# Expert rows gathered before the last scatter has landed, attention scores two units ahead, loads begun a stage early, and two scan states

## The reference

```python
# block one, chunks of 128 tokens: y = C @ (decayed state) + masked (C B^T * decay) @ (x dt)
states = einsum("bclgn,bcgrl,bclgrp->bcgrpn", bm, decay_states, xdt)
def step(h, inp):
    s, d = inp
    return h * d[..., None, None] + s, h        # the scan over chunks
y_diag = einsum("bcgls,bcgrls,bcsgrp->bclgrp", cb, lmat, xdt)
y_off = einsum("bclgn,bcgrpn,bcgrl->bclgrp", cm, prev, exp(a_cs))
# conformer: layer norm over 1024 channels: mean, variance, scale, silu
# block two, attention: softmax of the masked scores and a sink, per block of 128 queries
scores = where(valid, einsum('bnqgrd,bnkgd->bngrqk', q, kb) * HEAD_DIM**-0.5, NEG_INF)
out = einsum('bngrqk,bnkgd->bnqgrd', softmax(concat([scores, sink]))[..., :-1], vb)
h = layer_norm(DEEPNORM_ALPHA * x + concat([attn, sgu]) @ w_out + b_out)
# routed experts: rows sorted by expert into blocks of 128
x_rows = concat([xt, 0])[row_tok].reshape(n_blocks, 128, D)
def expert_block(xb, e):
    gt = minimum(xb @ w_gate[e] + b_gate[e], 7)
    up = clip(xb @ w_up[e] + b_up[e], -7, 7)
    hid = gt * sigmoid(1.702 * gt) * (up + 1.0)
    return hid @ w_down[e] + b_down[e]           # then weighed by the gate and summed per token
x = layer_norm(DEEPNORM_ALPHA * h + ffn)
```

## Time and profile before

| What | Value |
|---|---|
| Median of 3 runs | 3385.69 us (3377.62 to 3389.89) |
| The profiled execution | 3407.19 us |
| Its span | 3405.5 us |
| Mean granted TensorE clock | 0.962 of full speed |
| Busy share: TensorE, VectorE, ScalarE, GpSimd | 93%, 79%, 54%, 22% |
| Moved from and to HBM | 810 MB and 59 MB |

### The profile page before, as it was taken

One profiled execution on the slowest core, in us unless ns is written; L12 is line 12 of the kernel. 1 busy time (PEld: TensorE's weight loads), 2 busy tenths in 40 slices (PEclk: granted clock), 3 DMA queues, 4 the chain that ended last, 5 costly groups with the idle time before them and its releaser, 6 DMA issues. The chain is left out here.

```text
span 3405.5 us, 47872 instructions
## 1 busy us (share of the span) xinstructions
PE 3155.6 (93%) x16432; PEld 2732.6 (80%) x16432; DVE 2677.4 (79%) x3834; ACT 1822.1 (54%) x2211; POOL 750.4 (22%) x465
## 2 busy tenths in 40 slices
PE   7999788999887999999998958899999999999997
PEld 7996777999887888888887846787888788777775
DVE  6885552994596878887887555899999999999996
ACT  4432442334585333333333342677787777777774
POOL 0000002446211445454454000111111111111111
PEclk9999789999998999999999969899999999999998
DMA  5221031334457999999997113889999999999995
GB/s 143 71 75 38 1 124 66 136 118 170 179 204 274 335 349 350 348 349 345 347 328 274 72 53 136 334 333 347 363 359 358 356 356 369 341 356 364 342 359 201
DMA packets 195751, 853.26 MB, mean 251 GB/s; under 512 B 21776, under 2 KB 104336, under 8 KB 151936
## 3 DMA queue, kind: packets, MB, share of 16 engines
q1 hardware_dynamic: 167712, 700.86, 56.1%
q0 software_dynamic: 27936, 151.02, 10.9%
HBM read 810.39 MB, written 59.24 MB: 255 GB/s over the span
## 5 line engine op out<-in xcount | busy, mean ns | idle before, releaser
L3148 DVE TENSOR_TENSOR moe_w_lo<-all_raw,moe_w_hi 128x2048 fp32r<-128x2048 f32 x298 | 676.9, 2287 | 64.7 <-ACT moe_w_hi L3075 62.3
L3075 ACT ACTIVATE moe_w_hi<-all_raw 128x2048 fp32r<-128x2048 f32 x298 | 568.5, 1915 | 83.5 <-PE moe_GU L3014 60.1
L3014 PE MATMUL moe_GU<-moe_w_hi,moe_x_lo 128*128 128x512 f32 x1056 | 412.3, 390 | 0.0
L3013 PE MATMUL moe_GU<-moe_w_lo,moe_x_hi 128*128 128x512 f32 x1056 | 412.2, 390 | 0.0
L3012 PE MATMUL moe_GU<-moe_w_hi,moe_x_hi 128*128 128x512 f32 x1056 | 411.9, 390 | 0.0
L1230 POOL TENSOR_TENSOR score_w_lo<-all_hT,score_w_hi 128x1024 fp32r<-128x1024 f32 x67 | 165.3, 2468 | 673.6 <-DVE all_x_lo L1346 531.4
L1855 DVE SCALAR_TENSOR_TENSOR experts_pair<-experts_pair,all_x_first 128x1024 f32<-128x1024 f32 x128 | 156.2, 1220 | 133.3 <-DMA experts_pair<-in_peer_pairs,experts_slot 133.3
L1699 POOL DMA_INDIRECT experts_pair<-in_peer_pairs,experts_slot x128 | 225.1, 1759 | 114.7 <-POOL experts_slot L1696 110.1
L3013 PEld LDWEIGHTS moe_GU<-moe_w_lo,moe_x_hi 128*128 128x128 f32 x1056 | 198.8, 188 | 42.2
L3014 PEld LDWEIGHTS moe_GU<-moe_w_hi,moe_x_lo 128*128 128x128 f32 x1056 | 198.6, 188 | 41.6
L3012 PEld LDWEIGHTS moe_GU<-moe_w_hi,moe_x_hi 128*128 128x128 f32 x1056 | 199.0, 188 | 40.6
(11 more groups left out here) (542 smaller groups left out, 8077.3 us busy)
## 6 DMA issues: line engine op xcount, KB each, us to landing
all_raw<-in_w_moe SPq DMA_DIRECT2D x149, 2048.0 KB, 9.1
all_hT<-in_w_moe SPq DMA_DIRECT2D x49, 2048.0 KB, 9.4
all_hT<-in_peer_wdT SPq DMA_DIRECT2D x128, 512.0 KB, 5.4
all_wu<-in_peer_pairs SPq DMA_DIRECT2D x64, 1024.0 KB, 13.8
peer_gates<-gates_out SPq DMA_DIRECT2D x6, 4096.0 KB
experts_gt<-peer_gates SPq DMA_DIRECT2D x32, 768.0 KB
all_hT<-in_w_in SPq DMA_DIRECT2D x40, 512.0 KB, 4.4
all_hid<-peer_early SPq DMA_DIRECT2D x60, 192.0 KB
```

Source lines behind the costliest of these rows:

```text
L3013: pe.matmul(out, x_hi[:, kx, :], lo[:, k, :], start=False, stop=False)
L3014: mm = pe.matmul(out, x_lo[:, kx, :], hi[:, k, :], start=False, stop=(kx == KD - 1))
L3075: act.activation(w_hi[p % RING][:], piece_of(r, p), ACT.Copy).then_inc(w_high, 1)
L3148: dve.tensor_tensor(w_lo[p % RING][:], piece_of(r, p), w_hi[p % RING][:].bitcast(F32), ALU.subtract).then_inc(w_low, 1)
```

## The change

In the experts' stage GpSimd's wait for the landing of a scatter moves behind the next gather. The gather takes its indices from a small tile of its own (`source`); the slots for the scatter are copied later, and ScalarE waits for that copy (`filed`). The one-hot rows of the end are made by GpSimd, and three of VectorE's four additions move behind the split of the last result. In attention the scores run two units ahead with three buffers `sc`, and `b_out`, the first pair of output weights and h*ALPHA + b_out are loaded and computed there, in space of `c.hT`. In the scan `state` and `xdt` are double, the work between chunks is spread over the steps, `xw` and the sums of the conformer's squares go to GpSimd, and the first exponential waits for its own load alone.

```diff
-        xdt = s.sb("xdt", [P, HEADS, 64])
+        xdt = [s.sb(f"xdt{i}", [P, HEADS, 64]) for i in range(2)]
         xw = s.sb("xw", [P, HEADS, 64])
         btok = s.sb("btok", [P, GROUPS, P])
-        state = s.sb("state", [P, HEADS, 64])
+        state = [s.sb(f"state{i}", [P, HEADS, 64]) for i in range(2)]
...
+            @block.gpsimd
+            def _(pool):
+                def weigh_x(ch):
+                    n = cols(ch)[1]
+                    pool.wait_ge(xdt_ok, ch + 1)
+                    if ch >= 1:
+                        pool.wait_ge(st_done, ch)
+                    pool.tensor_tensor(xw[0:n, :, :], xdt[ch % 2][0:n, :, :],
+                                       keep[0:n, ch, :].unsqueeze(2).to_broadcast([n, HEADS, 64]), ALU.mult).then_inc(xw_ok, 1)
+                    pool.wait_ge(xw_ok, ch + 1)
+
+                def conf_add(i):
+                    pool.wait_ge(c_squared, i + 1)
+                    pool.tensor_tensor(csq[:, 0, :], csq[:, 0, :], csq[:, i, :], ALU.add).then_inc(c_added, 1)
+                    pool.wait_ge(c_added, i)
+
+                weigh_x(0)
+                weigh_x(1)
+                weigh_x(2)
+                for i in range(1, KD):
+                    conf_add(i)
+                weigh_x(3)
...
+                def conf_sums(first, end):
+                    for i in range(first, end):
+                        mm = pe.matmul(tot[:], c.ones[:], c.yT[:, KD + i, :], start=(i == 0), stop=(i == KD - 1))
+                    if end == KD:
+                        mm.then_inc(c_sum, 1)
+
+                conf_sums(0, 2)
...
-                    pe.wait_ge(c_squared, KD)
-                    for i in range(KD):
-                        mm = pe.matmul(c_sums[:, m:m + 1], csq[:, i, m * P:m * P + P], c.ones[:, 0:1],
-                                       start=(i == 0), stop=(i == KD - 1))
-                    mm.then_inc(c_sq_sum, 1)
+                    pe.wait_ge(c_added, KD - 1)
+                    pe.matmul(c_sums[:, m:m + 1], csq[:, 0, m * P:m * P + P], c.ones[:, 0:1],
+                              start=True, stop=True).then_inc(c_sq_sum, 1)
...
                 turn(0)
+                conf_sums(2, 4)
                 turn_b(0)
                 new_state(0)
+                conf_sums(4, KD)
                 turn(1)
                 decays(0)
+                turn_b(1)
...
-                    if g == 3 and ch < M:
-                        new_state(ch)
-                        turn(ch + 1)
-                    if n % 4 == 1 and ch < M:
-                        turn_b(ch)
+                    if ch < M:
+                        if g == 0:
+                            new_state(ch)
+                        if g == 2:
+                            turn(ch + 1)
+                        if g == 3 and ch + 1 < M:
+                            turn_b(ch + 1)
                     if n >= 3:
                         pe.wait_ge(dve_w, min(n + 2, 16))
                         if n == 9:
                             pe.wait_ge(c_var, 1)
                         square_sums(n - 3)
...
-                    if 5 <= n < 5 + M:
-                        conf_square_sums(n - 5)
+                    if n == 8:
+                        for m in range(M):
+                            conf_square_sums(m)
...
-                act.wait_ge(consts_in, 80)
+                act.wait_ge(alog_in, 16)
...
-                    dve.wait_ge(xdt_ok, ch + 1)
-                    dve.tensor_tensor(xw[0:n, :, :], xdt[0:n, :, :],
-                                      keep[0:n, ch, :].unsqueeze(2).to_broadcast([n, HEADS, 64]), ALU.mult).then_inc(xw_ok, 1)
...
+                    old, now = state[ch % 2], state[(ch + 1) % 2]
                     if ch == 0:
-                        dve.tensor_copy(state[:], new).then_inc(s_ok, 1)
+                        dve.tensor_copy(now[:], new).then_inc(s_ok, 1)
                         return
-                    step(dve.tensor_tensor(state[:], state[:], dec[:, ch, :].unsqueeze(2).to_broadcast([P, HEADS, 64]),
+                    dve.wait_ge(s_ok, ch)
+                    step(dve.tensor_tensor(now[:], old[:], dec[:, ch, :].unsqueeze(2).to_broadcast([P, HEADS, 64]),
                                            ALU.mult))
-                    dve.tensor_tensor(state[:], state[:], new, ALU.add).then_inc(s_ok, 1)
+                    dve.tensor_tensor(now[:], now[:], new, ALU.add).then_inc(s_ok, 1)
...
                         prepare(n + 1)
+                    if g == 3 and ch < M:
+                        take_x(ch + 1)
                     conf_work(n)
...
-                    if g == 3 and ch < M:
-                        take_state(ch)
-                        take_x(ch + 1)
+                    if ch < M:
+                        if g == 1:
+                            take_state(ch)
...
+    DEEP = 3
...
+                sp.dma_start(c.out_bias, a["b_out_2"].to_broadcast([P, D])).then_inc(bb_in, 16)
+                sp.dma_start(c.out_pair, rows(a["w_out_2"])[:, 0:2, :]).then_inc(c.pair_in, 16)
...
                 scores(0)
+                scores(1)
                 for i in range(UNITS):
-                    if i + 1 < UNITS:
-                        scores(i + 1)
+                    if i + 2 < UNITS:
+                        scores(i + 2)
...
-                    if i >= 2:
-                        dve.wait_ge(turned, 2 * i - 2)
+                    if i >= DEEP:
+                        dve.wait_ge(turned, 2 * (i - DEEP) + 2)
...
+                        h = c.h[:, i // 2, :]
+                        dve.wait_ge(bb_in, 16)
+                        dve.scalar_tensor_tensor(out=h, in0=h, scalar=ALPHA, in1=c.out_bias,
+                                                 op0=ALU.mult, op1=ALU.add).then_inc(pre_ok, 1)
...
-                sp.dma_start(bb[:], a["b_out_2"].to_broadcast([P, D])).then_inc(bb_in, 16)
-                for q in range(PAIRED):
+                sp.wait_ge(c.pair_in, 16)
+                sp.sem_inc(loaded[0], 16)
+                for q in range(1, PAIRED):
...
-                    pe.wait_ge(pre_ok, m + 1)
...
-                dve.wait_ge(bb_in, 16)
-                for m in range(M):
-                    dve.scalar_tensor_tensor(out=c.h[:, m, :], in0=c.h[:, m, :], scalar=ALPHA, in1=bb[:],
-                                             op0=ALU.mult, op1=ALU.add).then_inc(pre_ok, 1)
...
-                    pool.tensor_copy(slot[:, b, :], c.slots[:, ds(j, 1), :].rearrange("p o w -> p (o w)")).then_inc(slotted, 1)
+                    pool.tensor_copy(source[:, b:b + 1], c.slots[:, ds(j, 1), 0]).then_inc(slotted, 1)
                     pool.wait_ge(slotted, j + 1)
                     pool.sem_inc(paced, 1)
                     pool.indirect_dma_start(out=xg[:, b, :], out_offset=None, in_=c.h_rows[:, :],
-                                            in_offset=bass.IndirectOffsetOnAxis(ap=slot[:, b, 0:1].bitcast(U32), axis=0),
+                                            in_offset=bass.IndirectOffsetOnAxis(ap=source[:, b:b + 1].bitcast(U32), axis=0),
...
+                            pool.wait_ge(x_done, j + 1)
+                            pool.sem_inc(paced, 1)
                             gather(j + 1, 1 - u)
+                            pool.wait_ge(stored, j * 16 + 16)
+                            pool.sem_inc(paced, 1)
+                            pool.tensor_copy(slot[:, u, :], c.slots[:, ds(j, 1), :].rearrange("p o w -> p (o w)")).then_inc(filed, 1)
+                            pool.wait_ge(filed, j + 1)
+                            pool.sem_inc(paced, 1)
                             pool.wait_ge(y_ok, j + 2)
                             pool.sem_inc(paced, 1)
                             scatter(y[:, u, :], slot[:, u, 1:2]).then_inc(stored, 16)
-                            pool.wait_ge(stored, j * 16 + 16)
-                            pool.sem_inc(paced, 1)
...
+                pool.wait_ge(stored, n * 16)
+                pool.sem_inc(paced, 1)
                 pool.sem_inc(all_stored, 1)
+                pool.tensor_copy(token[:, 0:1], last[:, 0:1]).then_inc(token_ok, 1)
+                pool.wait_ge(token_ok, 1)
+                for m in range(1, M):
+                    pool.tensor_scalar(token[:, m:m + 1], token[:, 0:1], float(-P * m), None, ALU.add).then_inc(token_ok, 1)
+                pool.wait_ge(token_ok, M)
+                for m in range(M):
+                    pool.tensor_scalar(token_hot[:, m, :], c.count[:], token[:, m:m + 1], None,
+                                       ALU.is_equal).then_inc(hot_ok, 1)
+                pool.wait_ge(hot_ok, M)
...
+                            act.wait_ge(filed, j + 1)
...
-                step(dve.tensor_copy(token[:, 0:1], last[:, 0:1]))
-                for m in range(1, M):
-                    ins = dve.tensor_scalar(token[:, m:m + 1], token[:, 0:1], float(-P * m), None, ALU.add)
-                step(ins)
-                for m in range(M):
```

(11 more changed lines are left out.)

67 lines of the change are left out of this document (35 added, 32 removed).

## The result

| | median us | executions | lowest to highest |
|---|---|---|---|
| before | 3381.65 | 4 | 3374.72 to 3389.89 |
| after | 3331.04 | 4 | 3329.54 to 3333.81 |

The ratio is 0.985, 95% interval 0.9824 to 0.9876: 50.6 us less, between 42 and 60. The forecast was 3316, a gain of 69.7 from 3385.7, with a range of 3292 to 3346. The time lies in the range and on the side that the forecast gave 0.93 (faster by over 0.5%), 15 us above the forecast itself. The profiled execution of after took 3333.81 us (span 3332.1), against 3407.19 before: 73.4 less, where the sum had said 75. So the sum fits the two profiled executions and not the medians, and the study is mostly about that difference.

The account below looks back on a forecast made before the run. TensorE bounds the experts' stage; chains between engines bound attention and scan. 37 + 4.9 + 14 + 7.5 + 12 = 75 us off 3407.2 gave 3332 profiled; adjusted toward the median, 3316 us, range 3292 to 3346.

Parts of the forecast that it names:

- gathers (blocks): Experts' stage: gathers issued 12.4 us earlier remove TensorE's stalls and the clock loss behind them, 37 us (20 to 38).
- the end: Tail: one-hot rows on GpSimd and three additions behind the last split remove TensorE's wait, 4.9 us (3 to 5).
- attention + route: Attention: scores two ahead, 14 us (10 to 15); route: h and first weights ready, 7.5 us (4 to 9).
- scan: Scan: shorter gaps between chunks and sums off TensorE, less added waits and GpSimd's interference, 12 us (0 to 20).
- I take a quarter: Final sum: the median lay 21.5 us below the profiled execution; between 3310 and 3332 it chose 3316.
- the prediction's last part: Signs to look for: gather within 4 us of scatter, turn waits under 1 us, clock 1.00, periods near 35.9.
- dear case: Experts' stage: scatter and gather transfers strictly one after the other, gather's data taking 9.8 us after the scatter's landing.
- Rival (a): Experts' stage: the queue works whole transfers in turn, gathers give about 25 instead of 37 us, 3328; chance 0.12.
- 18.6 - 3 x 1.16: Attention: VectorE's 18.6 us of waits for scores, less additions taken over from the route stage, 15.1 us.
- 27.3 - 11.7 = 15.6 us saved: Scan: three gaps between chunks, 27.3 us, less VectorE's own work that stays in them, 15.6 us saved.
- The conformer's sums: Scan: TensorE's 64 instructions for them become 8, removing most of a 4.67 us VectorE delay, 4 us gain.
- VectorE's price for GpSimd: Scan: 18 us of GpSimd work lengthens VectorE's instructions, a cost of 0 to 18 us, taken as 5.

Follow-up runs that it names:

- before_again: The kernel before, unchanged, timed again to see what varies between its executions: 3378.3 us, ratio 1.0011.
- after_again: The changed kernel once more, unchanged, as base for other variants on its chip: 3328.2 us, ratio 0.9838.
- a_late: The changed kernel with only the order turned back, GpSimd waiting for the scatter's landing before it issues the gather: 3350.7 us, ratio 0.9907.
- a_conf_pe: The changed kernel with the conformer's sums of squares back on TensorE instead of GpSimd: 3335.8 us, ratio 0.9868.
- a_one_ahead: The changed kernel with attention's scores one unit ahead again instead of two, three score buffers kept: 3338.6 us.
- p3_scan: The kernel before with only the scan's part of the change: 3370.4 us, ratio 0.9977.
- a_h_first: The changed kernel with attention's four h additions put ahead of VectorE's wait for the spatial product: 3329.9 us, ratio 0.9850.
- a_h_pool: The changed kernel with attention's four h additions on GpSimd, each as a product and an addition, instead of VectorE: 3333.5 us.
- a_twice: The changed kernel with every gather issued a second time into a buffer that nothing reads: 3333.9 us, ratio 0.9864.
- p2_attention: The kernel before with only the attention and route part of the change: 3361.3 us, ratio 0.9946.
- p1_gathers: The kernel before with only the part for the earlier gathers and the tail's one-hot rows on GpSimd: 3354.7 us, ratio 0.9925.

## Why the prediction was right or wrong

The terms, against the two pairs of traces. The first pair has the execution on which the sum rested; the second pair, before_again and after_again, has usual ones. A row for attention ends at the route's first product, so it holds the idle time for h (8.02 us before, 1.42 after) that the prediction counted under the route:

| step of the prediction | forecast | first pair | second pair |
|---|---|---|---|
| gathers (blocks) | 37 | 39.2 | 18.4 |
| the end | 4.9 | 6.3 | 6.5 |
| attention + route | 14 + 7.5 | 20.2 + 3.3 | 14.2 + 2.9 |
| scan | 12 | 13.8 | 6.3 |
| sum | 75 | 82.8 | 48.3 |

**The step that failed is the one behind the sum:** "I take a quarter". I had seen that the profiled execution lay 21.5 us above the median and had named both explanations, a constant of profiling or more stalls than usual. It was the second, and not in the blocks alone: the profiled executions of the three parts lie within 2.5 us of their medians, the stalls in three more traces with the old gathers are 15.0 to 18.9 us against 28.3, and attention and scan were 6.4 and 4.3 us longer in that one execution as well. The gain in the blocks of the second pair is 18.4, of which 15.0 are stall and 3.4 clock. Had I taken all 21.5, the forecast would have been 3332, against 3331 measured; that this is so near is partly luck, as the terms below err in both directions. A stall made by the landing times of transfers is a quantity that varies, and it had a single sample.

**Gathers, mechanism: right.** Issue behind the scatter, no wait of the turn, clock 1.00, periods of 35.9 us in the mean (blocks 1 to 32: (3254.9 - 2142.3) / 31 = 35.9), weights in time, all as the prediction's last part asked; a_late shows that the order alone does it. The dear case was too dear: I let the gather's data come 9.8 us behind the scatter's landing, and in the 31 blocks where the gather follows its scatter at once the mean is 4.8, between 1.5 and 6.2. The two transfers overlap. The Trainium skill ("DMA: Bandwidth & Descriptors", section "Two DMAs through the same engine are not ordered") says that descriptors of one queue start in order but are pipelined; the trace agrees with the second half (1.5 us), and the first half does not lead to the dear case, as I had concluded from it. Rival (a), whole transfers in turn with 12.8 us between the landings, falls.

**The end: right, a little low.** 6.3 to 6.5 for 4.9: TensorE's wait for the split is gone, and the later work ran at a clock of 0.88 where it had 0.80. The one-hot rows cost GpSimd 6.28 us instead of VectorE's 3.06 and were hidden.

**Attention: right in kind, twice too high for a usual execution; route: too low.** Two units ahead give 6.9 us, not 14; without the idle time for h the rows above are 13.6 us in the first pair and 7.6 in the second. The term 18.6 - 3 x 1.16 came from the slower execution: in before_again VectorE's waits for scores are 14.4 us, of which the h additions fill about 4. Of the 10.2 left, 3.2 came back as another wait, for the spatial product, which I had named nowhere. The route's first product comes 1.42 us behind the stage's start where it had 8.02 idle, and the route itself is 2.9 to 3.3 shorter, its clock being 0.91 instead of 0.86: nearly 10 us for 7.5.

**Scan: the sum came out near by luck, both of its parts were wrong.** Between scans that begin at the same time the whole part is worth 9.5 to 10.6 us for a forecast of 12; the 13.8 and 6.3 of the table compare scans with different begins. "27.3 - 11.7 = 15.6 us saved" counted the gaps at a chunk's end as if the steps between were not bound by anything. In two of the three chunks' ends the work moved into steps that had no room, since one PSUM buffer still joined VectorE's state to TensorE's turn, and the turn stands in front of the next step's products. By a_conf_pe's 134.8 us all of it together is worth nothing without the sums (134.4 and 135.4 in the traces of the old scan that begin at the same 323.5 us). The conformer's sums, which I gave 4, are worth 10 beside it: that they stood in TensorE's queue at the chunk's end is where the traces show them, and why they cost so much more than their 4 us is argued, not shown. VectorE's price for GpSimd was about 4.4 us of longer instructions in after's trace, 5.4 in after_again's, for a forecast of 5.

## What to carry to other kernels

Before a sum is made against a profiled execution, put its time beside the spread of the others: where it lies at the edge, the waits on transfers in it are the edge's as well, and the gain to be had in the median is smaller by about the distance. Removing such a wait seems to narrow the spread as well (14 to 39 us in kernels with the wait, 4 to 15 in those without, though with fewer runs). A step taken out of a gap between two chunks is worth only what the steps that receive it have to spare: look which buffer and which queue still join them. And work handed to GpSimd can be paid for by VectorE even where VectorE's instruction has one input. The four additions lost by it, as VectorE was what their stage waited for; the conformer's sums won, as they left TensorE's queue.

## What was not expected of the hardware

The scan's length takes only a few values, and they follow the time at which it begins. It is 124.9 us in after and a_late, which begin it at 323.5 and 323.7, and 128.1 or 128.2 in after_again, a_one_ahead, p3_scan, a_h_first and a_h_pool, which begin it at 321.8 to 322.9; a_twice, at 324.1, has 126.5. The code of this stage is the same in all of them. The scan of the kernel before does the same: 138.7 us in before and p2_attention, which begin it at 321.7 and 322.1, 134.4 and 135.4 in before_again and p1_gathers, which begin it at 323.5. So the change is worth 9.5 or 10.5 us at the later begin and 10.5 or 10.6 at the earlier, while pairs with different begins show 6.3 or 13.8. What differs in their rows is where TensorE's granted clock stands at 0.5: 0.83 in the mean in after, 0.80 in after_again. That the begin is the cause is not tested, but it sorts all the traces. So a stage in which TensorE waits often can take 3 or 4 us more or less for a shift of 1 or 2 us in front of it, and a difference of that size in one trace says nothing about an edit.

GpSimd's `tensor_scalar` over 128 x 1024 took 2801 ns, VectorE's addition of the same size with a product in it 1225 (after_again). And 0.94 of the DMA engines' time, with 364 GB/s in after, was no limit yet: a_twice carried 8 MB more in the same 1120 us, 372 GB/s at 0.96, with no wait for weights.
